# A merged attention and delta-rule stage: value products ahead of the next scores, output turns together, turns held back for delta steps, and an end in another order

## What is computed

```python
proj = (rmsnorm(x, attn_norm) * (1 + scale_a) + shift_a) @ w_in
# head group A: causal attention, 8 heads, key = 64 plain + 32 rotary, value 64
s = einsum(q_nope, k_nope) + einsum(q_pe, k_pe); p = softmax(mask(s * scale)); o = p @ v
y_mla = rmsnorm(o, mla_out_norm)
# head group B: gated delta rule, 4 heads of 128, chunks; one step per chunk:
v_new = u - w @ state
o     = q_dec @ state + a_qk @ v_new
state = state * exp(g_last) + k_dec.T @ v_new
y_gdn = rmsnorm(o, gdn_out_norm) * silu(gate)
x = x + gate_a * (concat(y_mla, y_gdn) @ w_out)
# then routing, 32 experts (top 2 within the best group), final rmsnorm
```

## Time and profile before

| | us |
|---|---|
| three runs, median | 2417.65 (2413.59 to 2421.41) |
| profiled execution, its own time | 2419.23 |
| its span | 2417.5 |
| PE busy | 2182.2, 90% of the span |
| `mix`, from the first scores to the end of the last value products | 697.0 to 1455.4, 758.35 long |
| PE busy in it | 691.50 |

### The profile page before, as it was taken

One profiled execution on the slowest core, in us unless ns is written; L12 is line 12 of the kernel. 1 busy time (PEld: TensorE's weight loads), 2 busy tenths in 40 slices (PEclk: granted clock), 3 DMA queues, 4 the chain that ended last, 5 costly groups with the idle time before them and its releaser, 6 DMA issues. The chain is left out here.

```text
span 2417.5 us, 35480 instructions
## 1 busy us (share of the span) xinstructions
PE 2182.2 (90%) x11479; PEld 1243.3 (51%) x11480; DVE 987.8 (41%) x2202; ACT 872.1 (36%) x2123; POOL 631.6 (26%) x1108
## 2 busy tenths in 40 slices
PE   5999999999977998999999996999939999999990
PEld 2545555545444666666666673555534444444440
DVE  2334343433255575665566652234351222222223
ACT  2264363462655654555555561111111111111113
POOL 1000000000024542634542501233322222222224
PEclk9999999999988999999999998999969999999995
DMA  9212121120352344343343329333305788999777
GB/s 345 83 62 77 44 77 62 42 75 33 107 190 77 113 154 143 92 130 117 112 140 108 99 73 324 147 121 124 122 18 169 222 253 268 301 328 291 223 220 302
DMA packets 221896, 361.77 MB, mean 150 GB/s; under 512 B 45579, under 2 KB 143526, under 8 KB 218294
## 3 DMA queue, kind: packets, MB, share of 16 engines
q1 hardware_dynamic: 207926, 309.57, 37.6%
q0 software_dynamic: 13824, 50.34, 8.5%
HBM read 259.93 MB, written 99.93 MB: 149 GB/s over the span
## 5 line engine op out<-in xcount | busy, mean ns | idle before, releaser
L704 PE MATMUL pV<-keys_values_then_all,w_in_sb 128*128 128x512 f32 x768 | 341.3, 598 | 4.7 <-DMA w_in_sb<-in_w_in_dram 4.7
L2190 PE MATMUL hidden_ps<-w,keys_values_then_all 128*128 x752 | 331.5, 594 | 0.4 <-SPq L2062 0.4
L1252 ACT ACTIVATE probs<-scores,neg_max 128x512 f32<-128x512 f32 (+3 forms) x320 | 195.0, 621 | 227.6 <-DVE neg_max L1363 152.9
L704 PEld LDWEIGHTS pV<-keys_values_then_all,w_in_sb 128*128 128x128 f32 x768 | 145.1, 192 | 178.0 <-issue 177.3
L2190 PEld LDWEIGHTS hidden_ps<-w,keys_values_then_all 128*128 128x128 f32 x752 | 143.4, 191 | 180.6 <-issue 180.5
L1828 PE MATMUL out_ps<-keys_values_then_all 128*128 128x512 f32 x512 | 226.3, 601 | 2.5 <-ACT keys_values_then_all L1677 2.5
L2120 ACT ACTIVATE keys_values_then_all<-hidden_ps 128x256 f32<-128x256 f32 x47 | 18.0, 383 | 454.7 <-PE hidden_ps L2190 454.7
L2200 PE MATMUL expert_ps<-w_sb,keys_values_then_all 128*128 x368 | 169.8, 604 | 0.0
L1828 PEld LDWEIGHTS out_ps<-keys_values_then_all 128*128 128x128 f32 x512 | 97.2, 192 | 121.8 <-issue 116.2
L1169 POOL TENSOR_TENSOR keys_values_then_all<-keys_values_then_all 32x31 f32<-32x31 f32 (+15 forms) x248 | 120.5, 486 | 117.9 <-DMA keys_values_then_all<-a_d 98.7
L1508 PE MATMUL scores<-keys_values_then_all,queries 64*128 64x512 f32 (+3 forms) x640 | 148.0, 584 | 0.0
(11 more groups left out here) (371 smaller groups left out, 3196.6 us busy)
## 6 DMA issues: line engine op xcount, KB each, us to landing
w<-in_w_dram SPq DMA_DIRECT2D x64, 1024.0 KB, 10.4
w_sb<-in_w_dram SPq DMA_DIRECT2D x32, 1024.0 KB, 13.7
keys_values_then_all<-in_x_dram SPq DMA_DIRECT2D x32, 512.0 KB, 5.3
w_mod_rows<-in_w_mod_dram SPq DMA_DIRECT2D x16, 1024.0 KB, 4.9
keys_values_then_all<-in_w_mod_dram SPq DMA_DIRECT2D x4, 2048.0 KB, 15.0
qkv_d<-l_out SPq DMA_DIRECT2D x32, 256.0 KB, 2.3
keys_values_then_all<-y_d SPq DMA_DIRECT2D x16, 512.0 KB, 4.6
x_d<-keys_values_then_all SPq DMA_DIRECT2D x16, 512.0 KB, 2.9
```

What stands on the lines that cost most here:

```text
L704: last = pe.matmul(pV[n % 2][:], win[:, k, QKV0 + c * P:QKV0 + (c + 1) * P], hT[:, s % 2, k, :], start=(k == 0), stop=(k == ND - 1))
L1252: act.activation(prob[:, e, 0:w].rearrange("p t k -> p (t k)"), pS[e][:, 0:w * P], ACT.Exp, scale=-1.0, bias=nmin[:, i % 2, h, b:b + 1], a ...
L2190: last = pe.matmul(pH[par][:], xT[par][:, k], m.w13[:, ds(slot, 1), k].rearrange("p s n -> p (s n)"), start=(k == 0), stop=(k == ND - 1))
```

## The change

Within each group the atoms come in another order: both output turns stand right behind the transposes, then the value products, and only then the scores of the next group (before: one turn, next scores, value products, the other turn). A counter `cover` adds the cost of the delta steps since the last scores, and the transposes are not put into the list before it has reached 1.2 (`SCORE_COVER`). Delta steps held back (`O2`, `G`) are released behind an `S`, not behind a `V`. At the end of the stage, `BX` of the last tile goes ahead of `AS` of the tile before, and delta steps still held go ahead of the last `A`, `AS` instead of ahead of the atoms that are left. SP loads the gate of the next chunk at step `TR`, not at `O2`. In `output`, PE no longer waits for the routing weights and for `pick` before its first instruction, but where it first uses them.

```diff
         turns = [(0.13 * (TILE[i - 1] // 4 + 1), [("O", i - 1, hp)]) for hp in (2 * o, 2 * o + 1)] * (i > 0 and o < AH // 4)
-        atoms += turns[:1]
+        atoms += turns
+        atoms.append((0.65 * n, [("V", j, 0), ("V", j, 1)]))
         if ahead:
             atoms.append((0.8 * ahead, [("S", j + 1)] + [("X", j + 1, e) for e in range(4)]))
         if i and last and TILE[i] >= 4:
             atoms.append((0.0, [("AS", i - 1, 0)]))
-        atoms.append((0.65 * n, [("V", j, 0), ("V", j, 1)]))
-        atoms += turns[1:]
...
-    atoms.append((0.0, [("AS", NT - 2, 0), ("BX", NT - 1, 0), ("B2", NT - 1, 0)]))
+    atoms.append((0.0, [("BX", NT - 1, 0), ("AS", NT - 2, 0), ("B2", NT - 1, 0)]))
...
-    owed = 0.0
+    owed, cover = 0.0, SCORE_COVER
...
         order.append(step)
         owed += cost * share
+        cover += cost
         while atoms and owed >= atoms[0][0]:
+            kind = atoms[0][1][0][0]
+            if kind == "T" and cover < SCORE_COVER:
+                break
             owed -= atoms[0][0]
-            order += atoms[0][1]
-            if atoms.pop(0)[1][0][0] == "V":
+            order += atoms.pop(0)[1]
+            if kind == "S":
+                cover = 0.0
                 order += held
                 held = []
-    order += held
-    for _, kinds in atoms:
+    for _, kinds in atoms[:-1]:
         order += kinds
+    order += held + atoms[-1][1]
     return quads, order
...
+SCORE_COVER = 1.2
...
+                elif kind == "TR" and n + 1 < NT:
+                    wait(yg_stored, 16 * n)
+                    load_gate(n + 1)
...
                 elif kind == "O2":
-                    wait(yg_stored, 16 * n)
-                    if n + 1 < NT:
-                        load_gate(n + 1)
...
             pe.wait_ge(m.wo_loaded, 16 * 2)
-            pe.wait_ge(m.wr_loaded, 16 * 6)
-            pe.wait_ge(pick_made, 3)
...
+                    if n == 2:
+                        pe.wait_ge(pick_made, 3)
...
+                    else:
+                        pe.wait_ge(m.wr_loaded, 16 * 6)
```

## The result

The changed kernel takes 2524.09 us (median of 4 runs, 2523.18 to 2529.5) against 2416.38 for the kernel before (4 runs, 2413.59 to 2421.41) on the same chip. The ratio is 1.0444, with an interval of [1.0426, 1.0462]. The kernel is slower by 107.7 us where I predicted 45, and lies above my range. The profiled execution has a span of 2522.6 us against 2417.5, so 105.1 us have to be found.

What follows compares the result with a forecast made beforehand. PE was taken as the bound, busy 691.5 of the 758.35 us of `mix`. 2419.2 + 47.6 (waits) - 8.4 (end) + 4 (clock) = 2462.4, as median 2461; range 2412 to 2496, likeliest 2436 to 2485.

Steps and rivals of the forecast that it cites:

- the end: End of `mix` and start of `output`: 1.6 + 3.8 + 1.1 + 1.9 us saved, together -8.4 us.
- PE's clock: PE in `mix`: slightly lower granted clock from more idle time, +4 us, the low end of 0 to 38.
- the clock goes with the gaps: Rival: the first stretch's clock over the whole stage, up to +30 us, 2485 to 2510; chance 0.08.
- the waits of the new list: PE's idle time over all 80 groups of `mix`: 114.5 against 66.9 us, +47.6.
- the class of `K`: 13 groups with `K`, `KA` or bank-bound transposes and `KS` between scores and transposes: mean wait 1.6, together 21 us.
- join pair, 9 groups: `Y` and `WU` of level 2 before the transposes; `WU` waits for ACT's copy: mean 2.5, together 22.5 us.
- `TR`, 10 groups: `TR` between scores and transposes; `v_new` delays ACT's copies: mean wait 1.9, together 19 us.
- the banks' 8: Added in `mix` for bank and other small waits outside the class count, some 24 us before: +8 us.
- first 15 groups: Start of `mix`, mostly `I` steps giving PE no cover: mean wait 1.5, together 22.5 us.
- half the loss: Rival: stalls partly fall together, stage +6 to +27 us, end -8.4, 2415 to 2436; chance 0.2.
- The faster rival: Rival: delta steps hide exponentials, value products cover copies, the scores' 37.8 us go: 2371, or 2394 with half; chance 0.14.
- The join's line: Sign: L1469, the second join product, waits some 20 us for ACT's `Y_half`.

Runs made afterwards that it cites:

- The filler: Idle identity transposes before PE's waits: 632 in the changed kernel, 2487.4 us; 349 in the kernel before, 2402.32 us.
- scores first: Changed kernel with only the swap of value products and next scores undone, turns and hold kept: 2432.37 us, ratio 1.007.
- the first experiment: Kernel before plus only gate loads at `TR`, later waits in `output`, `BX` ahead of `AS`, held steps released last: 2417.52 us, ratio 1.0005.
- The half step: Kernel before with only the first half of the value products moved ahead of the next scores, in 53 groups: 2423.53 us, ratio 1.0034.

## Why the prediction was wrong

The direction and the mechanism were right, and both large terms were too small. Of the 61.9 us between the sum (47.6 - 8.4 + 4 = 43.2) and the 105.1 of the profiled executions, the waits account for 22.7, PE's busy time for 29.9, the end for 6.3, and what lies outside for 3.0.

**The step "PE's clock", +4, was about +20.** I took "the low end" of 0 to 38 because the first stretch differs from the rest in more than idle time, and gave the rival *the clock goes with the gaps* 0.08. It was this rival's mechanism that came, on top of waits that were larger too. `mix` ran at 0.94, and PE's busy time grew by 33.9 us, of which 1.6 is moved work. PE was busy at half clock for 91.5 us instead of 47.9; at 46% of loss that is 42 us instead of 22, so about 20 of the 33.9 are the clock (an estimate; at most 22, if half the clock at most doubles a row). The other 12 are not the clock. The prediction had nothing for them ("PE's work itself does not change"); pauses inside rows are one candidate, and no run separates it from others. The filler shows that the clock follows the idle stretches and not the longer stage: with them filled, both kernels run at 1.00, and the changed one is 36.7 us faster for doing 87.2 us more. The prediction used the Trainium skill (TensorE: Matmul & The Clock Gate, Part 1), by which the default is the throttled state and activity releases it. The filler agrees with that sentence (0.94 to 1.00 by activity alone). What was wrong is what I made of it, that short gaps in a busy stage would cost nothing; the sentence does not say so. I also wrote that no row of the kernel before shows such gaps. Its trace did: its 11 stretches at half clock stood behind a mean of 0.97 that I took for small. One of them follows the scores' wait of 1.96 us in the earlier trace rows:

```profile
1231.90:1235.30 3.40, 3.40 (x20) 2.47 (x18) 1.91 (x9) 1.93 (x8) 2.77 (x9) 0.50 0.02 5
```

**The step "the waits of the new list", +47.6, was +70.3.** I added up PE's idle times in the order of time for the same classes. The groups in them are not all the same: the class of `K` has 7 groups that the prediction had among the others.

| class | predicted | measured |
|---|---|---|
| join pair, 9 groups | 22.5 | 25.4 |
| `TR`, 10 groups | 19 | 16.8 |
| `K`, `KA`, `KS`: 13 groups predicted, 20 measured | 21 and the banks' 8 | 42.9 |
| others: 33 groups predicted (24 with waits), 26 measured | 21.5 | 26.1 |
| first 15 groups | 22.5 | 27.0 |
| together | 114.5 | 138.2 |

The sum on the right is within 1 us of the 137.2 of the stretch. Two classes were well sized, and two experiments bear them out: taking the join pair apart gave 21 us, moving `TR` gave 16 (each with some of the clock's share in it). The step that failed is the class of `K` with "mean 1.6" in 13 groups, and the "+8" for banks with it: 13.9 of the 23.7 us by which the right column is larger. 20 groups have such a step there, and they lose 2.1 us on average. 22.8 of their 42.9 us are waits for a bank that `qk_ahead` frees. Two things were missed. The prediction had DVE's queue (`G`, `O2`, `K`, `KA`) but followed it only to the copies; the rows of DVE above show it holding PE up earlier, at the banks of `K`, which the transposes (`KD`) and turns right behind want. And it priced `G` and `O2` at 1.14 us each, from a stretch in which POOL stood idle. Where POOL works on a piece of the inversion they take 2.3 to 2.6 us (`G`, 7 times of 16) and 2.3 to 3.0 (`O2`, 6 of 16) in the changed kernel, and the three longest waits for `qk_ahead` (4.90, 4.81, 3.57) all lie behind such a `G`, two of them behind such an `O2` too. The kernel before had these longer ones as well; the new list has PE wait behind them. That POOL's work is the cause is not shown by an experiment, only that the two go together. The hold was not in the prediction as a cost: it costs 21 us in the changed kernel, and the 16 us that remain with scores first are its own or the release's.

**The step "the end", -8.4, was -2.1.** The changes came as described: no wait for the gate is left, the weights' exponential precedes the scaling, PE starts 0.4 us after DVE. But I added up the waits that go and put the one that comes next at nothing: ACT writes a tile's output only when the store of the tile before has landed. The store of tile 13's attention went out at 1440.89 before, just ahead of the loads for `output`; now it stands behind them, and ACT waits 7.7 us for its landing. Even with that store ahead of the loads (the first experiment) ACT waits 6.94 us for the next one, the end is only 2.5 us sooner, and `output` gives that back.

**The rival *half the loss*** (a wait of PE lets ACT and DVE catch up) has no sign in its favour: the starts of the scores fall behind those of the kernel before steadily, by 17 us at group 15, 51 at group 46, 106 at group 78. The faster rival fell by the trace of waits: its condition was a mean idle time per group under 0.94 us, and it was 137.2/80 = 1.7.

**Signs named beforehand.** Scores' wait for copies gone: yes. Value products waiting 45 us and more: 64.1. The join's line about 20: 24.9. Transposes 15 or more: 14.7 shown in waits (13.7 for ACT), more inside their rows. `mix` about 805: 862.7. No gate wait at the end: right. PE's start about 2 us after the others' release: 0.4; this sign did not fit the prediction's own sum, which counts these 1.9 us as saved.

What stays open: what the 12 us of longer busy time are that the clock does not account for; what the hold and the new place of the release cost each; whether `G` and `O2` are slowed by POOL's work; and whether a list could be built that keeps the value products as cover and also removes the scores' 37.8 us. The half step tried (53 groups) lost 0.3%.

## What to carry to other kernels

Where two engines pass work to and fro, the products that stand between two dependent steps are what pays for the chain; moving them elsewhere removed one wait here and uncovered several others, so write the chain of the whole group with the queue of each engine, not the one wait that the move is for. Count idle time of the matrix engine twice: once as it stands, and once for the clock of the work behind it. Read a mean granted clock as time: 0.97 over 758 us was 51 us at half clock. Take the price of an instruction from a stretch in which the other engines do what they will do in the new order. If small waits can't be removed, cheap filler in them can be worth more than reordering (0.6% here). A large prefetch put ahead of a small store on one queue delayed the engine that waits for that store, and changing the order of the two here only changed which store it waited for.

## What the runs showed of the hardware

**Short pauses and the clock.** In the changed kernel's `mix` the granted clock fell to half 22 times, for 102.4 us together. At 21 of the 22 falls PE had just paused or was pausing, once or twice, for 1.8 to 7.2 us together; at 17 of the 22 no single pause was longer than 3.3 us. (Not every pause of such a length was followed by a fall.) The total of idle time is not what decides: 66.8 us went with 51.2 us at half clock in the kernel before, and 66 us with 3.4 in the changed kernel with filler. There the idle time was cut small: 5 pauses of 1.5 us or more, against 12 in the kernel before and 33 in the changed one.

**Work that saves time.** I had not expected that work added to the bounding engine makes the kernel faster: 349 idle transposes made the kernel before 14 us faster, 632 the changed one 36.7.

**DVE beside POOL.** DVE's four instructions of `G` took 1.13 to 1.14 us where POOL stood idle, and 2.3 to 2.6 us where POOL worked on a piece of the inversion; `O2` likewise. `K` (L1300) and the row minima (L1368), which read from PSUM, took the same with and without POOL's work: 0.34 and 0.68 us an instruction.

**Stores behind loads.** A store of 256 KB of attention output landed 2.0 us after its issue in the course of `mix` (median); behind the loads for `output`, ACT waited 6.9, 7.7 and 10.4 us for one in three kernels.
